# Moving two output tiles and three steps of cached values earlier in one TensorE order

## The reference, cut to what matters

```python
a = o_att @ w_att                                  # 256 -> 1024, attention branch
cb = silu(layer_norm(c)) @ w_conv_out              # convolution branch
h = sigmoid(ga) * a + sigmoid(gb) * cb
x = x + h @ w_out                                  # 1024 -> 1024
x = x + SwiGLU(RMSNorm(x))                         # width 2816
```

## Time and profile before

| | before |
|---|---|
| median of three runs | 1750.47 us |
| the profiled execution's own time | 1750.79 us |
| its span | 1749.0 us |
| TensorE matmul busy | 97% of the span |
| VectorE busy | 60% |
| ScalarE busy | 26% |
| mean share of the granted TensorE clock | 0.992 |

### The profile page before, as it was taken

One profiled execution on the slowest core, in us unless ns is written; L12 is line 12 of the kernel. 1 busy time (PEld: TensorE's weight loads), 2 busy tenths in 40 slices (PEclk: granted clock), 3 DMA queues, 4 the chain that ended last, 5 costly groups with the idle time before them and its releaser, 6 DMA issues.

```text
span 1749.0 us, 25445 instructions
## 1 busy us (share of the span) xinstructions
PE 1698.9 (97%) x10488; PEld 1577.3 (90%) x10488; DVE 1042.1 (60%) x1449; ACT 457.6 (26%) x900; POOL 70.7 (4%) x127
## 2 busy tenths in 40 slices
PE   5999999999999989999999999999999999999999
PEld 5899999999988879989777899989989989899897
DVE  5698898797999777586653424244342442433435
ACT  5111132323354455612222321111112111111110
POOL 0000000000000002120300000000000000000000
PEclk8999999999999999999999999999999999999999
DMA  6112253334424428984860122222222322222232
GB/s 203 49 42 60 60 174 122 97 98 136 149 74 168 146 91 268 313 301 158 298 213 1 37 97 71 87 97 97 97 93 80 105 97 85 74 95 97 97 114 101
DMA packets 155823, 211.56 MB, mean 121 GB/s; under 512 B 8362, under 2 KB 126474, under 8 KB 154939
## 3 DMA queue, kind: packets, MB, share of 16 engines
q1 hardware_dynamic: 145403, 134.01, 24.7%
q0 software_dynamic: 10320, 76.16, 12.0%
HBM read 180.04 MB, written 74.80 MB: 146 GB/s over the span
## 4 chain that ended last, share of the span: by engine, by line
PE 80%; DVE 9%; DMA 4%; DVEq 3%; issue 2%; ACT 1%; SPq 1%; ACTq 0%
PE ps L766 19%; PE ps L767 19%; PE ps L768 19%; PE ps L1243 5%; PE ps L1245 5%; PE ps L1244 5%; DVE conv L1612 3%; PE ps L1153 1%; PE ps L1155 1%; PE ps L1154 1%; PE ps L854 1%; DMA qb<-scr_q 1%; DMA sga<-scr_z 1%; SPq L535 1%; PE ps L979 1%
## 5 line engine op out<-in xcount | busy, mean ns | idle before, releaser
L766 PE MATMUL ps<-xhi,whi 128*128 128x352 f32 x1200 | 403.8, 337 | 1.6 <-DVE xlo L1587 1.6
L768 PE MATMUL ps<-xhi,wlo 128*128 128x352 f32 x1200 | 386.7, 322 | 0.0
L767 PE MATMUL ps<-xlo,whi 128*128 128x352 f32 x1200 | 386.3, 322 | 0.0
L766 PE MATMUL ps<-nhi,whi 128*128 128x352 f32 x1056 | 340.8, 323 | 0.8 <-DVE nlo L1975 0.8
L768 PE MATMUL ps<-nhi,wlo 128*128 128x352 f32 x1056 | 338.5, 321 | 0.0
L767 PE MATMUL ps<-nlo,whi 128*128 128x352 f32 x1056 | 338.5, 321 | 0.0
L1612 DVE SCALAR_TENSOR_TENSOR conv<-u,vec,conv 128x1024 f32<-128x1024 f32 x240 | 308.3, 1285 | 25.7 <-issue 11.2
L1568 DVE TENSOR_TENSOR wlo<-raw,whi 128x1024 fp32r<-128x1024 f32 x126 | 154.0, 1223 | 257.6 <-ACT whi L1334 249.4
L766 PEld LDWEIGHTS ps<-xhi,whi 128*128 128x128 f32 x1200 | 226.6, 189 | 11.6 <-issue 5.5
L767 PEld LDWEIGHTS ps<-xlo,whi 128*128 128x128 f32 x1200 | 227.1, 189 | 4.4
L768 PEld LDWEIGHTS ps<-xhi,wlo 128*128 128x128 f32 x1200 | 226.5, 189 | 0.0
(11 more groups left out here) (227 smaller groups left out, 1895.7 us busy)
## 6 DMA issues: line engine op xcount, KB each, us to landing
kv_sample<-cache_kv_w POOLq DMA_DIRECT2D x32, 1022.0 KB, 6.1
raw<-w_in SPq DMA_DIRECT2D x50, 512.0 KB, 4.6
raw<-w_gate_up SPq DMA_DIRECT2D x44, 512.0 KB, 3.8
scr_z<-zt SPq DMA_DIRECT2D x34, 528.0 KB, 3.2
qb<-scr_q POOLq DMA_DIRECT2D x24, 512.0 KB, 6.3
raw<-w_down SPq DMA_DIRECT2D x22, 512.0 KB, 4.1
kc<-cache_kv_w POOLq DMA_DIRECT2D x16, 512.0 KB, 7.2
kv_sample<-cache_kv_w POOLq DMA_DIRECT2D x8, 1016.0 KB, 6.4
```

The source lines that it names most:

```text
L766: pe_mm(out, wh, rhs_hi, start=first, stop=False)
L767: pe_mm(out, wh, rhs_lo, start=False, stop=False)
L768: return pe_mm(out, wl, rhs_hi, start=False, stop=last)
```

## The change

It is in two constants. The order of units gets output 0 ahead of the attention units of chunk 1 and output 1 in their middle, and the steps 0, 1 and 2 of cached values move to r = 8, 12 and 13. Steps 3 and 4 stay at r = 17 and 18, where output 2 still is at r = 18. Every wait is derived from these lists or stays as it is written, and the loads keep their place in their queues.

```diff
-    UNITS = [("att", c * KT + j) for c in range(2) for j in range(KT)] + [("out", t) for t in range(4)]
+    UNITS = [("att", j) for j in range(KT)] + [("out", 0)] + [("att", KT + j) for j in range(4)]
+    UNITS += [("out", 1)] + [("att", KT + j) for j in range(4, KT)] + [("out", 2), ("out", 3)]
     UNITS += [("att", 2 * KT + j) for j in range(KT)] + [("out", o) for o in range(4, DNG)]
...
-    VSTEP_AT = {10: 0, 15: 1, 16: 2, 17: 3, 18: 4}
+    VSTEP_AT = {8: 0, 12: 1, 13: 2, 17: 3, 18: 4}
     V_END = 18
```

## The result

Four runs of the changed kernel gave a median of 1777.39 us (1776.21 to 1779.14); four runs of the one before, 1750.64 us. The ratio is 1.0148, with a 95% interval of 1.0135 to 1.0160: slower, and 0.6 us from the forecast of 1778.0.

A forecast was written before the change was run, and what follows sets the result against it. TensorE, busy for 97% of the span, was taken as the bound. Waits and loads gave 24.3 us and the clock 3.2, together 27.5; on 1750.79 that gives 1778.3, with the median 0.3 lower: 1778.0 us, range 1769 to 1788.

The forecast's parts named there:

- 1: Before output 0: TensorE waits for 8 low parts, starts output 0 at 851.0 and stands still for 7.7 us.
- 2, 6: Output 0 to the end of cached-value step 2: 20.1 us without waits, plus 1.6 us of lowered clock.
- 3: VectorE's first residual waits for tile 0's input rows, loaded only after cached-value step 2: 5.1 us.
- 4: VectorE's backlog of gates, low parts and residuals, from first residual to 16th low part: 13.3 us.
- 5: Load of `va1` for cached-value step 3, issued 0.3 us after the last low part, taking 6.0 us.
- 6, 7: From cached-value step 3 on: 1.6 us of lowered clock after the long gap, otherwise work as before.
- fast loads: Rival: same mechanism, both loads at their fastest, 4.0 and 5.2 us, one half-clock stretch: 1774.6 us, chance 0.14.
- Step 7: After cached-value step 3 the order of work is as before, so the shift stays; total 27.5 us.
- Only the first wait: Rival: TensorE waits before output 0, but input rows come in time and VectorE isn't held up: 1756.4 us, chance 0.06.
- faster: Rival: output units cover VectorE, TensorE never waits, all 3.35 us come back: 1747.1 us, chance 0.02.

The follow-up runs named there:

- late_residual: The changed kernel with output 0's residual added only just before output 1's, so gates 8 to 11 go ahead of it: 1769.88 us, 1.0106 to before.
- early_rows: The changed kernel with step 2 reading v2 instead of v0, one load left out, tile 0's input rows loaded earlier: 1769.16 us, 1.0095 to before.
- other_data: The changed kernel with output 0 multiplying the attention result instead of h, so it waits for nothing: 1770.60 us, 1.0115 to before.
- no_va: The changed kernel with step 3 reading v7 instead of va1, whose load is left out: 1771.63 us, 1.0109 to before.
- filled: The changed kernel with 95 matmuls that nothing reads put in TensorE's three gaps: 1773.56 us, 1.0123 to before.
- no_waits: out1_back with output 0 on other data, waiting for no low part, and step 2 after r = 15: 1751.15 us, 0.9996 to before.
- steps_alone: The kernel before, old order of units, with only the new positions of the steps of cached values: 1755.09 us, 1.0020 to before.
- late_rows_step1: The kernel before with step 1 after attention 13 and input rows of tiles 0 and 2 loaded after step 3: 1750.88 us, 0.9997.
- out1_back: early_rows with output 1 moved back behind attention 15: 1762.17 us, 1.0055 to before.

## Why the prediction was right, step by step

| step | predicted, us | measured, us | from |
|---|---|---|---|
| 1: attention 0 to output 0 | 15.3 | 15.3 | 851.29 - 836.00 |
| 2, 6: output 0 to the end of step 2 | 20.1 + 1.6 | 22.9 | 872.32 + 1.85 - 851.29 |
| 3: rows of tile 0 | 5.1 | 3.7 | 877.84 - 874.17 |
| 4: residual to 16th low part | 13.3 | 13.6 | 891.44 - 877.84 |
| 5: load for step 3 | 6.3 | 4.2 | 895.68 - 891.44 |
| 6, 7: step 3 to attention 16 | 17.7 + 1.6 | 20.4 | 916.08 - 895.68 |

**The mechanism was right, and late_residual, early_rows, other_data and no_va show each link on the path.** That the size of the sum came out to 1 us (81.0 in the table's terms, 80.1 measured) is in part luck: errors of both signs met. Both loads were faster than taken, by 1.4 and 2.1 us, and at 3.5 and 3.9 us faster than the lowest ends that I had given, 4.0 and 5.2. The rival "fast loads" was right about them. The half clocks cost 2.6 and 2.7 us instead of 1.6 each. I had priced them from stretches behind gaps of 2.1 us; here the clock was 0.50 over the whole of the first 3.4 us behind the first gap and 0.76 over the rest of output 0. A long gap need not cost that much: in late_residual, behind the same gap, it was 0.58 over 3.4 us and then 1.00, a cost of 1.3. filled bears the 2.6 out for the first gap. The range that I gave ends at 1788 although its own sum goes to 1788.9; that didn't matter.

**Step 7** said that all of the shift stays. It gave 1.5 us back: behind the gap of 2.2 us before the rest of output 4 the clock didn't fall this time. The clock is again the third number from the end. First the changed kernel, then the one before:

```profile
931.00:936.00 5.00, 5.00 (x23) 4.03 (x23) 4.72 (x5) 3.94 (x5) 0.53 (x1) 1.00 0.95 297
```

```profile
904.13:909.13 5.00, 5.00 (x16) 3.92 (x16) 4.72 (x5) 3.93 (x5) 0.53 (x1) 0.66 0.96 306
```

**The gaps** were forecast at 7.7, 5.8 and 15 us and are 7.50, 4.33 and 10.36. The last is shorter mainly because attention 12 to 15 took 6.7 us at half clock and not 3.8, which uses up 2.9 us of the wait and doesn't move its end; the faster load is the other 2.1.

**A rival was mispriced.** "Only the first wait" had 1756.4 us. early_rows, which is just that condition, has 1769.2. The working left out that output 1 was the cover of step 3's load. The price of "faster" was too good as well, as far as no_waits can tell: output 0 doesn't wait there, and TensorE waits for loads before steps 2 and 3 instead. It isn't a clean test of that rival, since VectorE waits in it too. Neither was forecast, so the time didn't show it.

## What to carry to other kernels

Before moving a unit forward, list for every engine what stands in its queue behind the first wait of that unit: here one residual on VectorE held 8 gates, 4 of them with their inputs ready. Long work behind a slow producer is cover; moved ahead of the producer it covers nothing and inherits its wait. And where one point is set by a chain on another engine, as step 3 is here by VectorE and the load behind it, a better order on the busy engine may only move its idle time.

## What the runs showed of the hardware

- The same gap of 2.1 to 2.2 us on TensorE, before the rest of output 4, was followed by a granted clock of 0.66 over 5 us in the kernel before and of 1.00 in the changed one. All twelve profiled executions have this gap, with the same code around it. In four of them (the changed kernel, steps_alone, no_waits, late_rows_step1) the clock behind it was 1.00, and from attention 16 to the end they took 858.2 to 858.5 us; in the other eight it was 0.66 to 0.74 over 5 us, and they took 859.7 to 860.0. A short gap thus costs 0 or about 1.5 us, by what looks like chance; this is as large as the effects that the last experiments looked for. TensorE: Matmul & The Clock Gate (Part 1: The HAM clock gate) in the Trainium skill says that the window in which activity is judged runs freely and doesn't start with the kernel, which fits; no run here tests it.
- After gaps of 7.5 us the half clock cost between 1.3 and 2.6 us over one output unit of 5.75 us (7.1 us in late_residual, 7.9 in early_rows, 8.1 in out1_back, 8.2 in no_va, 8.4 in the changed kernel). Behind the wait for step 3 the way to attention 16 was 1.4 (other_data) to 2.7 us (the changed kernel) longer than the 17.7 us of before, for gaps of 7.1 to 11.7 us. The cost did not grow with the gap: the longest gave the least.
- The 512 KB load of tile 0's input rows took 9.1 us with five others around it, 3.5 us in the changed kernel with one other issued right behind it, and 17.0 us in no_waits, where it was issued 0.4 us behind a gate load of 1408 KB and beside value loads.
